# Half of a depthwise convolution moved from VectorE to TensorE, with shifted copies of its input stacked on the partitions

## The chip, the cores and the metric

One core of one Trainium2 chip runs the whole program. The metric is the device time of one execution in microseconds (us), as the median over runs.

## The reference, cut to what matters

The program chains two transformer-like blocks over 256 tokens with 2048 channels. The second block has four layers; the third of them (one of four) mixes with a gated convolution along the tokens. Only that layer is touched:

```python
def conformer_conv_mix(h, w_in, dw_w, dw_b, ln_g, ln_b, w_out):
    a, a_gate, z = jnp.split(h @ w_in, 3, axis=-1)          # 2048 -> 3 x 2048
    g = a * jax.nn.sigmoid(a_gate)
    # depthwise: 31 taps along the tokens, one weight per tap and channel, pad 15
    y = lax.conv_general_dilated(g, dw_w[:, None, :], (1,), [(15, 15)], ..., 
                                 feature_group_count=2048) + dw_b
    y = jax.nn.silu(layer_norm(y, ln_g, ln_b))
    return (y * jax.nn.silu(z)) @ w_out
```

## The kernel before, in words

Channels lie on the 128 partitions, in 16 blocks of 128 channels, and the 256 tokens lie on the free axis. All large projections run alike. The weights come from HBM in slabs of 1 MB (128 partitions x 2048 float32), four slabs to a *group* of four output blocks. SyncE loads each slab into one of four `raw` buffers. Every product is made to nearly float32 precision from three fp32r matmuls: ScalarE casts the slab to `whi` (L942, two buffers, so that the cast of a slab waits until the slab two places earlier has been multiplied), VectorE subtracts to get `wlo` (L1372), and TensorE runs 48 matmuls per slab (L456, L457, L458: high x high, high weights x low input, low weights x high input), 192 per group. The instruction order of each engine is written out by hand, and semaphores tie the engines together.

In the convolution layer the first projection is called `ci` and has 12 groups. Groups 0 to 7 each give two channel blocks of `a` and two of `a_gate`; ScalarE makes the sigmoid (L1314) and VectorE the product, into `gp` (L1973, `drain_ci`), which is padded by 15 zero tokens on both sides. Groups 8 to 11 give `z`. The convolution is done by VectorE alone, in 16 blocks x 31 taps = 496 instructions on 128 x 256 elements: `conv_steps` yields them two blocks at a time, and `conv_some(17)` puts 17 of them behind the drain, behind the third and behind the fourth weight subtraction of every group:

```python
for g in range(1, 12):
    split(r, g, 0)
    split(r, g, 1)
    if g <= 8:
        drain_ci(g - 1)
    conv_some(17)
    split(r, g, 2)
    conv_some(17)
    split(r, g, 3)
    conv_some(17)
```

When group 10 has been multiplied, TensorE sums the convolved blocks over the channels for the layer norm (L867, plain float32 matmuls with a matrix of ones); it waits there for all 16 blocks (`s_conv`). Then follow group 11, the sum of squares (L875), the normalization, and the projection `co`. GpSimd only issues DMAs: the modulation weights `w["ada"]`, 512 KB each (L430), which VectorE sums (L1398) in those stages that have `ada` work; `ci` has none.

Of the kernel before, what the change touches and what calls it, by code (L numbers as in the profile page):

```python
# [21 lines left out]
ACT = mybir.ActivationFunctionType  # L22
# [128 lines left out]
def build(nc, w, vec, out):  # L151
    ctx = ExitStack()
    with ctx:
# [3 lines left out]
        def sb(name, cols, dt=F32, at=None):  # L157
            nonlocal base
            if at is None:
                at = base  # L160
                base += (cols * 4 + 31) // 32 * 32
            place[name] = at
            return nc.alloc_sbuf_tensor_at(name, [P, cols], dt, offset=at)

        def sem(name):
            return ctx.enter_context(nc.semaphore(name))
# [67 lines left out]
        kc = tiles(sb("kc", 4 * T, at=arena + 36864))  # L234
        vx = tiles(sb("vx", 2 * T, at=arena + 40960))
        vc = tiles(sb("vc", 2 * T, at=arena + 43008))
        PADT = T + 30
        gp_t = sb("gp", KT * PADT, at=arena)
        gp = gp_t[:, :].rearrange("p (k n) -> p k n", n=PADT)
        zs_t = sb("zs", KT * T, at=arena + KT * PADT * 4)  # L240
# [1 line left out]
        yc_t = sb("yc", KT * T, at=arena + KT * PADT * 4 + 16384)  # L242
        yc = tiles(yc_t)
        k2 = sb("k2", K2_N, at=arena + 52224)
        assert arena + 52224 + K2_N * 4 <= 229368 and base <= 229368, (base, arena)
        dft = k2[:, K2_DFT:K2_DFT + 1024].rearrange("p (k n) -> p k n", k=2)
        chan = k2[:, K2_CHAN:K2_CHAN + 512].rearrange("p (k n) -> p k n", k=2)
# [72 lines left out]
        s_f2 = sem("dft_even_odd_ready")  # L320
        s_fe = sem("dft_even_copied")
        s_fb = sem("dft_combined")
        s_cg = sem("conv_gates_ready")
        s_conv = sem("conv_done")
        s_lnq = sem("conv_squares_ready")
# [21 lines left out]
        def gate_halves(r, q):  # L347

            n = 8 * (2 + r["extra"])
            return range(min(n, (3 + (not r["extra"])) * q // 2), min(n, (3 + (not r["extra"])) * (q + 1) // 2))  # L350

        def gate_sums(r, q):

            return [h // 8 for h in gate_halves(r, q - 3) if h % 8 == 7] if q >= 3 else []

        def conv_squares(c):
            return (sq[:, 0:1024], sq[:, 1024:2048], pt[:, :], sq[:, 0:1024])[c]
# [59 lines left out]
        @block.gpsimd  # L417
        def _(pool):
            nc.gpsimd.memset(ones[:, :], 1.0).then_inc(s_const, 1)

            def load(a, i, both):

                per = 4 if both else 2
                if i >= 2:
                    pool.wait_ge(s_acc, ada_at(a, both) + per * (i - 1))
                elif not isinstance(a, int) or a:
                    before = both or isinstance(a, int)
                    pool.wait_ge(s_acc, ada_at(a, both) - ((4 if before else 2) * (1 - i) + (not before)))
                pool.dma_start(aslab[:, i % 2, :, :].rearrange("p k n -> p (k n)"),  # L430
                               w["ada"][a, i // 2, :, 1024 * (i % 2):1024 * (i % 2) + 1024])\
                    .then_inc(s_araw[i % 2], 16)

            def group(a, both):
                for i in range(8):
                    load(a, i, both)
            group(0, True)
            with pool.Fori(1, ADA_BOTH) as a:
                group(a, True)
            group(ADA_BOTH, False)  # L440
            with pool.Fori(ADA_BOTH + 1, ADA_GROUPS) as a:
                group(a, False)

# [3 lines left out]
        def _(pe):  # L448
# [409 lines left out]
            project("ao", "ya")  # L858

            norm("nci")  # L860
            project("ci", "nci", n=10)
            project("ci", None, g0=10, n=1)

            for c in range(4):
                pe.wait_ge(s_conv, 4 * c + 4)
                for k in range(4):
                    last = nc.tensor.matmul(bank[5][:, 0:T], ones[:, :], yc[:, 4 * c + k, :],  # L867
                                            start=c == 0 and k == 0, stop=c == 3 and k == 3)
            last.then_inc(s_lns, 1)
            project("ci", None, g0=11, n=1)  # L870

            for c in range(4):
                pe.wait_ge(s_lnq, c + 1)
# [61 lines left out]
        def _(act):  # L935
            def split(r, g, s):
                act.wait_ge(s_raw[s], (g + (r["m0"] + 1)) * 16)
                n = r["width"]
                m = g * SLABS + (SLABS * r["m0"] + s)
                if not (isinstance(m, int) and m < 2):  # L940
                    act.wait_ge(s_slab, m - 1)
                nc.scalar.copy(whi[:, s % 2, 0:n], raw[:, s, 0:n]).then_inc(s_hi, 1)  # L942
# [365 lines left out]
            def drain_ci(r, g, par):  # L1308
                summed(r, g)
                if g < 8:  # L1310

                    if g >= 2:
                        act.wait_ge(s_drain, 2 * (r["e0"] + g - 1))
                    nc.scalar.activation(sq[:, 1024 * (g % 2):1024 * (g % 2) + 512],  # L1314
                                         bank[2 * par + 1][:, :], ACT.Sigmoid).then_inc(s_cg, 1)
                else:
                    if g == 8:

                        act.wait_ge(s_drain, 2 * (r["e0"] + 8))
                    for half in range(2):  # L1320
                        at = 1024 * (g - 8) + 512 * half
                        last = nc.scalar.activation(zs_t[:, at:at + 512], bank[2 * par + half][:, :],
                                                    ACT.Silu)
                    last.then_inc(s_drain, 2)
            split(r, 0, 2)
            split(r, 0, 3)
            for g in range(1, 12):
                split(r, g, 0)
                split(r, g, 1)
                drain_ci(r, g - 1, (r["e0"] + g - 1) % 2)  # L1330
                split(r, g, 2)
                split(r, g, 3)
            for c in range(4):
                act.wait_ge(s_lnr, c + 1)
                if c == 3:
                    act.wait_ge(s_lns, 2)
                nc.scalar.activation(conv_squares(c), yc_t[:, 1024 * c:1024 * c + 1024],
                                     ACT.Square).then_inc(s_lnq, 1)
                if c == 2:
                    drain_ci(r, 11, (r["e0"] + 11) % 2)  # L1340
# [18 lines left out]
        def _(dve):  # L1359
# [577 lines left out]

            def conv_steps():

                for k in range(0, KT, 2):  # L1940
                    for t in range(TAPS):
                        for b in (k, k + 1):
                            x = gp[:, b, t:t + T]
                            wt = col("conv_dw_w_2", 16 * t + b)
                            yield b, t, x, wt
# [33 lines left out]
            for g in range(1, 12):  # L1979
                split(r, g, 0)  # L1980
                split(r, g, 1)
                if g <= 8:
                    drain_ci(g - 1)
                conv_some(17)
                split(r, g, 2)
                conv_some(17)
                split(r, g, 3)
                conv_some(17)
            dve.wait_ge(s_lns, 1)
            mu = sc[:, 512:768]  # L1990
            link(v.tensor_scalar(mu, bank[5][:, 0:T], 1.0 / D, None, ALU.mult))
# [58 lines left out]
def host_weights(a):  # L2050
# [47 lines left out]
    out["wao"] = slabs_of(a["attn_w_out_2"][0], full)  # L2098
    ci = [c for g in range(8) for c in (256 * g, 256 * g + P, D + 256 * g, D + 256 * g + P)]
    out["wci"] = slabs_of(a["conv_w_in_2"][0], ci + run_of(2 * D, 16))  # L2100
    out["wco"] = slabs_of(a["conv_w_out_2"][0], full)
    return out

# [90 lines left out]
```

## Time and profile before

| what | us |
|---|---|
| median of 3 runs (lowest, highest) | 3667.39 (3663.97, 3670.04) |
| the profiled execution, its own time | 3667.97 |
| its span in the trace | 3666.3 |
| TensorE matmul busy / share | 3333.8 / 91% |
| VectorE busy / share | 2686.8 / 73% |
| granted TensorE clock, mean | 0.945 |
| groups 1 to 10 of `ci` | 2873.6 to 3172.0 |

### The profile page before, as it was taken

The numbers are of one execution on the slowest core, as the hardware profiler recorded it, in microseconds if no ns is written. First come the engines' busy times: TensorE is split into PE (matmuls) and PEld (weight loads), VectorE is DVE, ScalarE is ACT, GpSimd is POOL, SyncE is SP. The second block draws the span as 40 slices with busy tenths as digits, with TensorE's granted clock in tenths as the row PEclk, the third lists the DMA queues.
The fourth block names the chain that finished last, engine by engine and source line by source line (L and its number), as shares of the span: only waits on it lengthen the run. The fifth ranks groups of instructions, "written<-read, shape, count | busy, mean of one in ns | idle before, by whom it ended". The sixth has DMA issues, their size and how long they took to land.

```text
span 3666.3 us, 59897 instructions
## 1 busy us (share of the span) xinstructions
PE 3333.8 (91%) x24466; PEld 3131.4 (85%) x24466; DVE 2686.8 (73%) x3615; ACT 1371.6 (37%) x1506; POOL 203.6 (6%) x389
## 2 busy tenths in 40 slices
PE   5999788999998789989999999898999888989998
PEld 5999657989996569979999999897779878889998
DVE  7887777888886778876767576566776899767554
ACT  3333334343333343343333334433553322344332
POOL 0000000000000000000100010000000000000000
PEclk9999878999998779999999999999999999999999
DMA  5777304757776017756776675574007344456753
GB/s 207 260 262 255 134 12 161 253 199 265 262 261 209 23 59 263 253 197 226 254 260 223 212 260 202 176 268 174 1 12 264 127 139 139 147 197 222 236 186 137
DMA packets 124954, 696.51 MB, mean 190 GB/s; under 512 B 14136, under 2 KB 14288, under 8 KB 66128
## 3 DMA queue, kind: packets, MB, share of 16 engines
q1 hardware_dynamic: 67392, 484.47, 38.3%
q0 software_dynamic: 55296, 201.35, 15.4%
q10 hardware_dynamic: 2064, 7.78, 0.6%
q8 instruction: 152, 2.49, 0.3%
q14 instruction: 50, 0.41, 0.0%
HBM read 691.43 MB, written 2.10 MB: 189 GB/s over the span
## 4 chain that ended last, share of the span: by engine, by line
PE 72%; DVE 18%; ACT 4%; issue 3%; DMA 3%; ACTq 0%; DVEq 0%; POOLq 0%
PE bank L456 19%; PE bank L457 18%; PE bank L458 18%; DVE wlo L1372 4%; DVE yc L1962 4%; DMA aslab<-w_ada_dram 2%; ACT whi L942 2%; PE bank L559 2%; DVE acc L1398 2%; PE bank L853 2%; PE bank L550 1%; DVE sc L1531 1%; PE bank L790 1%; PE bank L769 1%; PE bank L834 1%
## 5 line engine op out<-in xcount | busy, mean ns | idle before, releaser
L456 PE MATMUL bank<-uhi,whi 128*128 128x256 f32 x6784 | 1960.1, 289 | 180.0 <-DVE wlo L1372 89.6
L457 PE MATMUL bank<-ulo,whi 128*128 128x256 f32 x6784 | 1941.3, 286 | 0.0
L458 PE MATMUL bank<-uhi,wlo 128*128 128x256 f32 x6784 | 1940.2, 286 | 0.0
L942 ACT CAST whi<-raw 128x2048 fp32r<-128x2048 f32 (+1 forms) x464 | 875.6, 1889 | 1786.1 <-PE bank L458 1710.7
L1372 DVE TENSOR_TENSOR wlo<-raw,whi 128x2048 fp32r<-128x2048 f32 (+1 forms) x464 | 1054.0, 2273 | 649.1 <-ACT whi L942 648.9
L456 PEld LDWEIGHTS bank<-uhi,whi 128*128 128x128 f32 x6784 | 1325.0, 195 | 196.7 <-issue 129.0
L457 PEld LDWEIGHTS bank<-ulo,whi 128*128 128x128 f32 x6784 | 1325.9, 195 | 1.0
L458 PEld LDWEIGHTS bank<-uhi,wlo 128*128 128x128 f32 x6784 | 1324.3, 195 | 0.0
L1398 DVE SCALAR_TENSOR_TENSOR acc<-aslab,sm,acc 128x512 f32<-128x512 f32 x1008 | 695.9, 747 | 58.1 <-DMA aslab<-w_ada_dram 57.7
L430 POOL DMA_DIRECT2D aslab<-w_ada_dram x384 | 203.2, 529 | 3299.0 <-DVE acc L1398 2528.6
L1962 DVE SCALAR_TENSOR_TENSOR yc<-gp,cols,yc 128x256 f32<-128x256 f32 x480 | 193.3, 489 | 0.0
L559 PE MATMUL bank<-sq,ones 128*128 128x256 f32 x160 | 47.6, 461 | 39.7 <-ACT sq L1022 39.7
L1295 ACT ACTIVATE sc<-sc,sm 128x512 f32<-128x512 f32 x64 | 46.2, 722 | 96.7 <-DVE sm L1901 96.7
L494 PE MATMUL bank<-whi,uhi 128*128 128x512 f32 (+1 forms) x192 | 71.0, 370 | 10.9 <-DVE wlo L1372 7.9
L1169 ACT ACTIVATE sc<-sc,sm 128x256 f32<-128x256 f32 x84 | 42.0, 501 | 101.8 <-DVE sm L1757 101.8
L559 PEld LDWEIGHTS bank<-sq,ones 128*128 128x128 f32 x160 | 36.7, 236 | 47.6 <-issue 31.2
L1505 DVE RECIPROCAL sc<-sc 128x256 f32<-128x256 f32 x10 | 17.5, 1753 | 79.2 <-ACT sc L1030 79.2
L1893 DVE SCALAR_TENSOR_TENSOR sc<-bank,k 128x512 f32<-128x512 f32 x64 | 44.3, 692 | 40.1 <-PE bank L836 40.1
L496 PE MATMUL bank<-wlo,uhi 128*128 128x512 f32 (+1 forms) x192 | 69.6, 363 | 0.0
L498 PE MATMUL bank<-whi,ulo 128*128 128x512 f32 (+1 forms) x192 | 69.4, 361 | 0.0
L550 PEld LDWEIGHTS bank<-ones,asum 128*128 128x128 f32 x576 | 69.0, 192 | 0.4
L550 PE MATMUL bank<-ones,asum 128*128 128x1 f32 x576 | 67.0, 243 | 0.0
(249 smaller groups left out, 2607.7 us busy)
## 6 DMA issues: line engine op xcount, KB each, us to landing
aslab<-w_ada_dram POOLq DMA_DIRECT2D x384, 512.0 KB, 5.3
raw<-w_win_dram SPq DMA_DIRECT2D x96, 1024.0 KB, 5.0
raw<-w_wfi_dram SPq DMA_DIRECT2D x96, 1024.0 KB, 5.7
raw<-w_wfo_dram SPq DMA_DIRECT2D x48, 1024.0 KB, 5.0
raw<-w_wci_dram SPq DMA_DIRECT2D x48, 1024.0 KB, 4.9
raw<-w_wo_dram SPq DMA_DIRECT2D x32, 1024.0 KB, 4.9
raw<-w_wpg_dram SPq DMA_DIRECT2D x32, 1024.0 KB, 5.2
raw<-w_wqz_dram SPq DMA_DIRECT2D x32, 1024.0 KB, 5.1
```

The lines of the kernel that those rows point to most:

```text
L430: pool.dma_start(aslab[:, i % 2, :, :].rearrange("p k n -> p (k n)"), w["ada"][a, i // 2, :, 1024 * (i % 2):1024 * (i % 2) + 1024])\
L456: nc.tensor.matmul(o, whi_, xhi_, start=start, stop=False, skip_group_check=True)
L457: nc.tensor.matmul(o, whi_, xlo_, start=False, stop=False, skip_group_check=True)
L458: return nc.tensor.matmul(o, wlo_, xhi_, start=False, stop=stop, skip_group_check=True)
L494: nc.tensor.matmul(o, uhi[:, kt, tk], whi[:, s % 2, wc], start=kt == 0, stop=False, skip_group_check=True)
L550: last = nc.tensor.matmul(o, asum[:, c, P * b:P * (b + 1)], ones[:, 0:1], start=True, stop=True, skip_group_check=True)
L559: last = nc.tensor.matmul(bank[7][:, 0:T], ones[:, :], squares(c)[:, T * k:T * (k + 1)], start=c == 0 and k == 0, stop=c == 3 and k == 3)
L853: last = nc.tensor.matmul(o, v, p[:, P * c:P * (c + 1)], start=c == 0, stop=c == 3, skip_group_check=True)
L942: nc.scalar.copy(whi[:, s % 2, 0:n], raw[:, s, 0:n]).then_inc(s_hi, 1)
L1372: v.tensor_tensor(wlo[:, s, 0:n], raw[:, s, 0:n], whi[:, s % 2, 0:n].bitcast(F32), ALU.subtract).then_inc(s_lo, 1)
L1398: ins = v.scalar_tensor_tensor(out=out, in0=x, scalar=silu, in1=before, op0=ALU.mult, op1=ALU.add)
L1962: ins = v.scalar_tensor_tensor(out=yc[:, b, :], in0=x, scalar=wt, in1=yc[:, b, :], op0=ALU.mult, op1=ALU.add)
```

## The change

Of every four channel blocks, VectorE keeps the first two (0, 1, 4, 5, 8, 9, 12, 13) and TensorE takes the other two (`PE_BLOCKS`: 2, 3, 6, 7, 10, 11, 14, 15).

For each of TensorE's blocks GpSimd issues 17 DMAs: one of 512 KB from HBM with the tap matrices, made on the host (`wcv`), and 16 from SBUF to SBUF of 32 partitions x 284 float32 (36 KB), which write four copies of `gp`, shifted by 0, 1, 2 and 3 tokens, below one another on the partitions, once for each quarter (32 channels) of the block. A contraction over the 128 partitions then covers four taps of 32 channels. TensorE multiplies in 8 steps of four taps with four matmuls each (one per quarter, 128 x 32 weights, 256 tokens, plain float32), each writing its own 32 partitions of the same PSUM bank (6 or 7): 32 matmuls per block. The buffers for taps and shifted copies are double. ScalarE copies the result to `yc` and adds the bias. A block is multiplied behind the second and another behind the fourth slab of groups 3, 5, 7 and 9; TensorE's groups are no longer in a hardware loop there. VectorE's share per group goes from 17+17+17 to 10+9+9 instructions. GpSimd's loop over the modulation loads is cut in two, and the loads for `co` are issued after those of the convolution.

```diff
-        PADT = T + 30
+        PADT = T + 32
+        SHIFT = T + 28
+        shifted = [k2[:, K2_AX:K2_AX + 4 * SHIFT], zs_t[:, 2048:2048 + 4 * SHIFT]]
+        taps = [pt[:, :], sc[:, 0:1024]]
+        PE_BLOCKS = [4 * (i // 2) + 2 + i % 2 for i in range(8)]
 # GpSimd
-            with pool.Fori(ADA_BOTH + 1, ADA_GROUPS) as a:
+            with pool.Fori(ADA_BOTH + 1, RUN["co"]["a0"]) as a:
+                group(a, False)
+            pool.wait_ge(s_nl, 16 * (U_NORMS["nci"] + 1))
+            for i, b in enumerate(PE_BLOCKS):
+                if i >= 2:
+                    pool.wait_ge(s_cp, i - 1)
+                pool.dma_start(taps[i % 2], w["wcv"][i]).then_inc(s_cl_[i % 2], 16)
+                pool.wait_ge(s_drain, 2 * (RUN["ci"]["e0"] + b // 2 + 1))
+                for j in range(4):
+                    for c in range(4):
+                        pool.dma_start(shifted[i % 2][32 * j:32 * j + 32, SHIFT * c:SHIFT * (c + 1)],
+                                       gp[32 * c:32 * c + 32, b, j:j + SHIFT]).then_inc(s_cl_[i % 2], 16)
+            with pool.Fori(RUN["co"]["a0"], ADA_GROUPS) as a:
                 group(a, False)
 # TensorE
-            project("ci", "nci", n=10)
-            project("ci", None, g0=10, n=1)
+            def conv_block(i):
+                pe.wait_ge(s_cl_[i % 2], 16 * 17 * (i // 2 + 1))
+                if i >= 2:
+                    pe.wait_ge(s_cc, i - 1)
+                for q in range(8):
+                    for c in range(4):
+                        at = 32 * (4 * q + c)
+                        last = nc.tensor.matmul(bank[6 + i % 2][32 * c:32 * c + 32, 0:T],
+                                                taps[i % 2][:, at:at + 32],
+                                                shifted[i % 2][:, SHIFT * c + 4 * q:SHIFT * c + 4 * q + T],
+                                                start=q == 0, stop=q == 7, skip_group_check=True)
+                last.then_inc(s_cp, 1)
+            def behind(g, s):
+                if g in (3, 5, 7, 9) and s % 2:
+                    conv_block(g - 3 + s // 2)
+            for g in range(11):
+                group(r, g, (r["e0"] + g) % 2, slab_t, "nci" if g == 0 else None,
+                      lambda s, g=g: behind(g, s))
             for c in range(4):
-                pe.wait_ge(s_conv, 4 * c + 4)
+                pe.wait_ge(s_conv, 2 * c + 2)
+                pe.wait_ge(s_cc, 2 * c + 2)
 # ScalarE
+            def conv_copy(i):
+                act.wait_ge(s_cp, i + 1)
+                b = PE_BLOCKS[i]
+                nc.scalar.activation(yc[:, b, :], bank[6 + i % 2][:, 0:T], ACT.Identity,
+                                     bias=col("conv_dw_b_2", b)).then_inc(s_cc, 1)
             for g in range(1, 12):
                 split(r, g, 0)
                 split(r, g, 1)
+                if g in (4, 6, 8, 10):
+                    conv_copy(g - 3)
                 drain_ci(r, g - 1, (r["e0"] + g - 1) % 2)
                 split(r, g, 2)
                 split(r, g, 3)
+                if g in (3, 5, 7, 9):
+                    conv_copy(g - 3)
 # VectorE
-                for k in range(0, KT, 2):
+                for k in range(0, KT, 4):
                     for t in range(TAPS):
                         for b in (k, k + 1):
...
-                conv_some(17)
+                conv_some(10)
                 split(r, g, 2)
-                conv_some(17)
+                conv_some(9)
                 split(r, g, 3)
-                conv_some(17)
+                conv_some(9)
```

## Rows read from the trace of the kernel before

**Rows 1.** The page: span, busy engines, shares of the chain that ended last.

```profile
span 3666.3 us, 59897 instructions
PE 3333.8 (91%) x24466; PEld 3131.4 (85%) x24466; DVE 2686.8 (73%) x3615; ACT 1371.6 (37%) x1506; POOL 203.6 (6%) x389
...
PE 72%; DVE 18%; ACT 4%; issue 3%; DMA 3%; ACTq 0%; DVEq 0%; POOLq 0%
```

**Rows 2.** Stretches: an `in0` group, `ci` group 0, groups 1 to 10, one group, L867, tail.

```profile
core 0: us, PE busy (x) PEld busy (x) DVE busy (x) ACT busy (x) POOL busy (x), PEclk, DMA share, GB/s
184.00:207.00 23.00, 23.00 (x195) 23.00 (x194) 18.24 (x19) 7.03 (x6) 1.72 (x4) 1.00 0.73 265
2847.30:2873.60 26.30, 25.58 (x195) 25.41 (x196) 17.69 (x26) 10.76 (x15) 0.00 (x0) 0.91 0.35 120
2873.60:3172.00 298.40, 249.89 (x1920) 244.65 (x1919) 289.17 (x544) 84.87 (x54) 0.00 (x0) 0.95 0.41 141
2934.00:2964.20 30.20, 25.30 (x192) 24.69 (x192) 29.56 (x57) 8.11 (x5) 0.00 (x0) 0.94 0.41 140
3172.00:3179.00 7.00, 7.00 (x35) 6.17 (x34) 2.29 (x1) 2.88 (x3) 0.00 (x0) 1.00 0.46 152
3202.10:3224.70 22.60, 6.91 (x32) 5.74 (x32) 16.73 (x13) 19.22 (x27) 0.00 (x0) 0.75 0.14 46
```

**Rows 3.** Waits in `ci` groups 1 to 10 (us in total, times, longest).

```profile
ACT whi L942 <- PE bank L458: 211.7, 40, 8.5
...
PE bank L456 <- DVE wlo L1372: 45.4, 24, 2.9
DVE wlo L1372 <- ACT whi L942: 8.2, 9, 3.5
```

**Rows 4.** VectorE in order of time, over one group of `ci` (start us, us).

```profile
2966.17 2.29 DVE L1372 TENSOR_TENSOR wlo<-raw,whi 128x2048 fp32r<-128x2048 f32 x1 [0.65 <-ACT whi L942]
2968.38 0.69 DVE L1973 TENSOR_TENSOR gp<-bank,sq 128x512 f32<-128x512 f32 x1
2968.98 6.82 DVE L1962 SCALAR_TENSOR_TENSOR yc<-gp,cols,yc 128x256 f32<-128x256 f32 x17
2975.70 2.29 DVE L1372 TENSOR_TENSOR wlo<-raw,whi 128x2048 fp32r<-128x2048 f32 x1
...
2993.42 2.30 DVE L1372 TENSOR_TENSOR wlo<-raw,whi 128x2048 fp32r<-128x2048 f32 x1
2996.43 2.29 DVE L1372 TENSOR_TENSOR wlo<-raw,whi 128x2048 fp32r<-128x2048 f32 x1 [0.71 <-ACT whi L942]
```

**Rows 5.** TensorE in order of time around L867.

```profile
3171.77 0.28 PE L457 MATMUL bank<-ulo,whi 128*128 128x256 f32 x1
3171.89 0.28 PE L458 MATMUL bank<-uhi,wlo 128*128 128x256 f32 x1
3172.01 7.07 PE L867 MATMUL bank<-yc,ones 128*128 128x256 f32 x32
3178.72 0.47 PE L456 MATMUL bank<-uhi,whi 128*128 128x256 f32 x1
```

**Rows 6.** TensorE at 466 us: the first two index heads, float32, 64 partitions each.

```profile
466.92 1.14 PE L625 MATMUL bank<-zz 64*128 64x256 f32 x8 [2.61 <-DVE an L1563]
```

**Rows 7.** TensorE: one-column matmuls, each with its own 128x128 weights.

```profile
3273.53 0.95 PE L550 MATMUL bank<-ones,asum 128*128 128x1 f32 x8
```

**Rows 8.** TensorE in the attention, where the shape of the tile changes.

```profile
2660.38 0.60 PE L853 MATMUL bank<-pt,vc 128*64 128x128 f32 x4
2660.91 0.70 PE L834 MATMUL bank<-kx,zq 64*128 64x256 f32 x2
2661.45 0.59 PE L836 MATMUL bank<-kc,zq 64*128 64x256 f32 x2
2661.97 0.66 PE L843 MATMUL bank<-kk,sc 128*128 128x128 f32 x4
```

**Rows 9.** GpSimd: its two DMAs back to back, and DMA issues of the page.

```profile
1.42 1.19 POOL L430 DMA_DIRECT2D aslab<-w_ada_dram  x2 [0.34 <-issue]
...
aslab<-w_ada_dram POOLq DMA_DIRECT2D x384, 512.0 KB, 5.3
```

**Rows 10.** ScalarE in order of time: casts around the end of `ci` group 3.

```profile
2964.24 1.90 ACT L942 CAST whi<-raw 128x2048 fp32r<-128x2048 f32 x1 [8.38 <-PE bank L458]
2966.04 0.59 ACT L1314 ACTIVATE sq<-bank 128x512 f32<-128x512 f32 x1
2971.68 1.91 ACT L942 CAST whi<-raw 128x2048 fp32r<-128x2048 f32 x1 [5.04 <-PE bank L458]
```

**Rows 11.** Smallest ScalarE operation of the shape that the new copy has.

```profile
2840.76 0.47 ACT L1030 ACTIVATE sc<-bank,sm 128x256 f32<-128x256 f32 x1 [1.96 <-PE bank L559]
```

**Rows 12.** SyncE's loads during one `ci` group.

```profile
q1 hardware_dynamic: 576, 4.19, 40.6%
...
raw<-w_wci_dram SPq DMA_DIRECT2D x4, 1024.0 KB, 4.9
```

More of the change, by code:

```diff
@@ L244, in build @@
         k2 = sb("k2", K2_N, at=arena + 52224)
+        SHIFT = T + 28
+        shifted = [k2[:, K2_AX:K2_AX + 4 * SHIFT], zs_t[:, 2048:2048 + 4 * SHIFT]]
+        taps = [pt[:, :], sc[:, 0:1024]]
+        assert K2_AX + 4 * SHIFT <= K2_N and KT * PADT * 4 + 2 * 16384 <= 52224
         assert arena + 52224 + K2_N * 4 <= 229368 and base <= 229368, (base, arena)
@@ L322, in build @@
         s_fb = sem("dft_combined")
+        s_cl_ = [sem(f"conv_shifts_and_taps_loaded{i}") for i in range(2)]
+        s_cp = sem("conv_block_multiplied")
+        s_cc = sem("conv_block_copied")
         s_cg = sem("conv_gates_ready")
@@ L860, in _ @@
             norm("nci")
-            project("ci", "nci", n=10)
-            project("ci", None, g0=10, n=1)
+            r = RUN["ci"]
+            def conv_block(i):
[16 more added lines that the diff above has]
+                      lambda s, g=g: behind(g, s))
             for c in range(4):
-                pe.wait_ge(s_conv, 4 * c + 4)
+                pe.wait_ge(s_conv, 2 * c + 2)
+                pe.wait_ge(s_cc, 2 * c + 2)
                 for k in range(4):
@@ L869, in _ @@
             last.then_inc(s_lns, 1)
-            project("ci", None, g0=11, n=1)
+            group(r, 11, (r["e0"] + 11) % 2, slab_t)
             for c in range(4):
@@ L1319, in drain_ci @@
                         act.wait_ge(s_drain, 2 * (r["e0"] + 8))
+                    if g == 10:
+                        act.wait_ge(s_cp, 8)
                     for half in range(2):
@@ L2100, in host_weights @@
     out["wci"] = slabs_of(a["conv_w_in_2"][0], ci + run_of(2 * D, 16))
+    dw = np.asarray(a["conv_dw_w_2"][0])
+    taps = np.zeros((8, P, 8, 4, 32), dw.dtype)
+    lane = np.arange(32)
+    for i in range(8):
+        b = 4 * (i // 2) + 2 + i % 2
+        for t in range(dw.shape[0]):
+            for c in range(4):
+                taps[i, 32 * (t % 4) + lane, t // 4, c, lane] = dw[t, P * b + 32 * c + lane]
+    out["wcv"] = taps.reshape(8, P, 1024)
     out["wco"] = slabs_of(a["conv_w_out_2"][0], full)
```

## The prediction

> **What bounds the kernel now.** The page says that TensorE is the fullest engine and holds 72% of the chain that ended last, VectorE 18% [rows 1]. An average does not say who is late in `ci`, so the stretches come next. The bound elsewhere is an `in0` group: 192 fp32r matmuls, each 0.12 us behind the last [rows 5], take 192 x 0.12 = 23.04 us, and the stretch shows TensorE busy for all of its 23.0 us [rows 2]. Groups 1 to 10 of `ci` take 298.4 us instead of 230.4, at a clock of 0.95 instead of 1.00, and VectorE is busy for 289.2 of them (97%) [rows 2]. The waits agree: TensorE waits 45.4 us for `wlo` from VectorE, while VectorE waits 8.2 us for anything [rows 3]. The rest of the 68.0 us (298.4 - 230.4) is restarts and slabs that run at the lower clock after a wait. So `ci` is bound by VectorE, and 68.0 us is all that a lighter VectorE can give back there.
>
> VectorE's group of 30.2 us is, by starts in [rows 4], four subtractions at 2.21 us (8.8), one drain at 0.60 and 51 convolution steps at 6.72/17 = 0.396 us (20.2), with about 0.6 of waiting: 29.6 + 0.6. The pitch of 0.396, not the duration, is the price, since the instructions overlap.
>
> **What is removed.** 248 of 496 steps x 0.396 = 98 us of VectorE. A group's load becomes 8.8 + 0.6 + 28 x 0.396 (11.1) = 20.5 us, under TensorE's 23.04. Work is left for 248/28 = 8.9 groups, so VectorE ends in group 9, before L867. The later a subtraction may come counts too: a cast takes 1.9 us and a subtraction 2.3 behind the end of the slab two back, and TensorE needs it 5.76 us (23.04/4) after that end. A chunk of 10 steps (4.0) plus one subtraction (2.2) is 6.2, 0.4 over 5.76, and the chunks of 9 are 5.8; the 1.5 us in hand absorbs both. The `in0` stretch has almost this load, 18.2 us busy on VectorE in gaps of 2.7 us, and shows no TensorE idle [rows 2]. So the bound passes to TensorE, and I let VectorE's steps cost nothing behind it; should that cover fail, rival C prices it. For restarts and uneven chunks I allow 0.25 us a group, 2.5 us; this is a choice, about the size of one late restart (0.31 us from L456 to L457 after L867 where 0.12 is the rule).
>
> **What is added on TensorE.** This is the term that decides. Eight blocks of 32 float32 matmuls, two records each, are 64 records a block. A float32 record of 256 tokens starts 6.71/31 = 0.216 us after the last at clock 1.00 [rows 2, 5]. If the four 32-column tiles take turns, a block is 64 x 0.216 = 13.8 us; if all four run at once, 16 x 0.216 = 3.5 us, a pitch of 0.054 us per record. The trace has no adjacent column tiles. It has row tiles: heads 0 and 1 of L625 sit on partitions 0 to 63 and 64 to 127, and their 8 records take 1.14 us with the last one's 0.38 inside, (1.14 - 0.38)/7 = 0.109 us of pitch, half of 0.216 [rows 6]. So float32 matmuls on different parts of the array do overlap. Against a full factor of four stand the weights: 8 one-column matmuls, each with a fresh 128-column load, have a pitch near (0.95 - 0.25)/7 = 0.10 us [rows 7], which would make 64 records 6.4 us; here a load is 32 columns, a quarter. Bounds of the block are thus 3.5 and 13.8, with 6.4 between them. I take a pitch of 0.066 us (4.2 us), close to the end of four at once, because the nearest row [rows 6] halves exactly and the load shrinks with its columns. Changing the tile shape costs about 0.1 us each way: L834 begins 0.20 us after the last record of L853 where that one's pitch is 0.11 [rows 8]; with the first, longer matmul I add 0.3. A block is 4.5 us, eight are 36 us, all on the path, since nothing else can run on TensorE.
>
> The Trainium skill (TensorE: Matmul & The Clock Gate, Measured speedup vs the span model) reports 2.38x for three column tiles of 32 columns; that is 79% of full, and an estimate from the page at the same share would be 3.2x for four, 4.4 us for 64 records. No run here shows column tiles yet; by the page the sum would be 2 us longer.
>
> **What is added elsewhere.** ScalarE gets eight copies of about 0.5 us [rows 11] in a stretch where it is busy 85 of 298 us [rows 2]. In line behind a copy stand the sigmoid, the drain and the next cast; the copy of an odd block waits for the block that TensorE runs first anyway, so the cast behind it is due only after another 5.76 us slab [rows 10]. Nothing. The other end, 8 x 0.5 = 4 us, is inside the range.
>
> GpSimd issues 17 DMAs a block, idle otherwise. Two 512 KB DMAs back to back took 1.19 us together, so 0.66 a piece [rows 9]; for 17, 11 us, plus a landing of at most 5.3 [rows 9]. A pair of blocks is needed once in two groups, 46 + 9 = 55 us. Blocks 2 and 3 are drained about 5 us into group 2 and wanted 11.5 and 23 us into group 3: 29 us for the first, against 11 + 5. Hidden up to about 1.4 us per DMA (34 x 1.4 + 5.3 + some 2 for the waits between = 55). The `ada` loads for `co` come behind them on GpSimd's queue, in group 9 at the latest, over 40 us before `co` wants them. The transfers add 8 x (0.5 + 0.57) = 8.6 MB to queues at 41% in this stage [rows 12]; `in0` ran at 73% without delaying TensorE [rows 2]. Nothing. Group 0 (26.3 us), L867 (7 us), group 11 and the tail (22.6 us with TensorE mostly idle) [rows 2] stay.
>
> **Sum.** Groups 1 to 10: 230.4 + 36.0 + 2.5 = 268.9 us against 298.4, 29.5 us less. The profiled execution had 3667.97 us, 1.7 outside its span of 3666.3, and lies 0.6 above the median, so the difference is taken from the median: 3667.4 - 29.5 = 3638 us (-0.8%). Break-even is a block of 65.5/8 = 8.2 us, a pitch of 0.123, or 1.75 tiles at once.
>
> **Rivals.**
> - A, column tiles take turns (slower). Each matmul uses all 128 partitions, so the load for the next tile or the stream of the moving operand could exclude the other tiles; the only overlap seen is between different partitions [rows 6]. Then a block is 13.8 + 0.3 = 14.1, eight 113 us: 230.4 + 113 + 2.5 = 346, 47 us more, 3715 us. It decides from 8.2 us per block. For it: no row shows column tiles side by side. Against: the array's parts do work independently. The Trainium skill (TensorE: Matmul & The Clock Gate, The mechanism) states that weight loads overlap running matmuls only when the row group differs, which speaks for this rival; here loads of 0.19 us run under matmuls of the same rows at a pitch of 0.12, so the trace does not bear it out for whole tiles. Chance 0.13.
> - B, they overlap by halves, or the weight loads set the pace at 0.10 to 0.11: a block of about 7 us, 56 us in all, 10 us faster, 3658 us. Chance 0.12.
> - C, VectorE stays late: its in-order chunks delay subtractions by 0.5 us on each of the 40 slabs, 20 us of the gain: 3656. The `in0` stretch speaks against it. Chance 0.06.
> - D, GpSimd's gathers are late. From 1.4 us per DMA the 34 of a pair exceed the 55 us, and each further 0.1 us costs 4 x 3.4 = 14 us; at 1.6 the gain is gone, at 2 it is 6 x 14 - 29.5 = 54 us slower, 3722. Against: 0.66 for larger ones [rows 9]. For: no SBUF to SBUF DMA of this size is in the trace. Chance 0.06, half of it slower.
>
> The forecast, 0.63. Its own range is a block of 3.8 to 5.5 us with 0 to 4 us of waits: 3630 to 3648.
>
> **How the numbers follow.** Faster by over 0.2% (7.3 us, about what a measurement of this kernel can tell from no change, its runs spreading over 6): 0.63 + 0.10 of B + 0.06 of C + 0.01 of D = 0.80. Slower: A 0.13, D 0.03 = 0.16. Between: 0.04. The low end of the range is the full factor of four and no waits, 230.4 + 8 x 3.6 = 259, 39 us less: 3628. The high end takes in B and C, 3660, and leaves A and most of D out.
>
> **What would show it.** Right: the records of the new matmuls at a pitch of 0.05 to 0.08 us, blocks of 4 to 5.5 us, no wait of TensorE on `wlo` over 1 us in even groups, VectorE near 20.5 us busy per group, L867 about 29 us earlier, GpSimd done with a block before TensorE asks. Wrong: a pitch of 0.2 (A) or 0.1 (B), waits on `wlo` (C), a wait on a DMA in front of a block (D), or a clock below 1.00 in `ci`, which would stretch everything on TensorE.

## The result

| | before | changed |
|---|---|---|
| median, us (lowest to highest) | 3668.7 (3663.97 to 3670.04, 4 runs) | 3621.11 (3613.81 to 3624.17, 4 runs) |
| ratio of the times, 95% interval | | 0.987 (0.9852 to 0.9887) |
| the profiled execution, its own time / span | 3667.97 / 3666.3 | 3622.15 / 3620.5 |
| mean granted TensorE clock | 0.945 | 0.949 |

Faster, as forecast, but by 47.6 us where 29.5 were worked out: the time lies below the low end of the range (3628). The direction and the place were right, two terms were too dear, and some microseconds came from outside the stage, where the prediction counted nothing.

**Where the time went.** The page of the changed kernel, for [rows 1]: VectorE has lost 97 us of work, and its share of the chain has fallen from 18% to 13%.

```profile
span 3620.5 us, 60788 instructions
PE 3340.4 (92%) x24978; PEld 3130.4 (86%) x24978; DVE 2589.8 (72%) x3367; ACT 1375.8 (38%) x1514; POOL 270.6 (7%) x525
...
PE 79%; DVE 13%; ACT 3%; issue 3%; DMA 2%; ACTq 0%; DVEq 0%; POOLq 0%
```

Stretches of the changed kernel, for [rows 2]: group 0 of `ci`, and groups 1 to 10 with the eight blocks.

```profile
core 0: us, PE busy (x) PEld busy (x) DVE busy (x) ACT busy (x) POOL busy (x), PEclk, DMA share, GB/s
2839.50:2865.90 26.40, 25.49 (x195) 25.35 (x196) 17.78 (x26) 10.87 (x15) 0.53 (x1) 0.92 0.40 140
2865.90:3126.50 260.60, 260.60 (x2433) 246.60 (x2433) 192.76 (x296) 88.62 (x63) 67.60 (x137) 1.00 0.61 198
```

Groups 1 to 10 take 260.6 us instead of 298.4, TensorE is busy for all of them, and the clock is 1.00 where it was 0.95. The queues moved 198 GB/s and TensorE waited for none of it. Behind it stand the matmuls of the layer norm (L910, L867 before), as in [rows 5]:

```profile
3126.24 7.07 PE L910 MATMUL bank<-yc,ones 128*128 128x256 f32 x32
```

The waits in that stretch, for [rows 3]: TensorE has none, for `wlo` or for a DMA; its weight loads show 3.3 us of issue, the rest are waits of engines that have time. VectorE's for ScalarE went from 8.2 to 66.6 us: it is now the one that waits.

```profile
engine line waited for: us in total, times, longest us
ACT whi L985 <- PE bank L480: 162.4, 41, 5.5
POOL k L461 <- DVE gp L2027: 92.4, 4, 42.8
DVE wlo L1426 <- ACT whi L985: 66.6, 21, 7.3
POOL pt L457 <- PE bank L893: 55.2, 3, 20.4
ACT yc L1375 <- PE bank L893: 13.3, 8, 1.7
PEld bank L478 <- issue: 3.3, 8, 0.4
```

**The price of a block.** ScalarE casts once per slab, so the pitch of its casts is the time of a slab, and of a slab with a block behind it. ScalarE in order of time (start us, us):

```profile
2917.69 1.90 ACT L985 CAST whi<-raw 128x2048 fp32r<-128x2048 f32 x1 [3.36 <-PE bank L480]
2923.45 1.90 ACT L985 CAST whi<-raw 128x2048 fp32r<-128x2048 f32 x1 [3.85 <-PE bank L480]
2927.01 0.48 ACT L1375 ACTIVATE yc<-bank,cols 128x256 f32<-128x256 f32 x1 [1.67 <-PE bank L893]
2932.99 1.90 ACT L985 CAST whi<-raw 128x2048 fp32r<-128x2048 f32 x1 [5.50 <-PE bank L480]
```

2923.45 - 2917.69 = 5.76 us is a bare slab; 2932.99 - 2923.45 = 9.54 is one with a block: the block costs **3.78 us**. TensorE over the same block:

```profile
2923.08 0.28 PE L480 MATMUL bank<-uhi,wlo 128*128 128x256 f32 x1
2923.28 3.66 PE L893 MATMUL bank<-k,pt 128*32 128x256 f32 x64
2926.88 0.39 PE L478 MATMUL bank<-uhi,whi 128*128 128x256 f32 x1
2927.10 0.28 PE L479 MATMUL bank<-ulo,whi 128*128 128x256 f32 x1
```

Its first four records alone, in a shorter stretch:

```profile
2923.28 0.42 PE L893 MATMUL bank<-k,pt 128*32 128x256 f32 x4
```

64 records with the last one's 0.38 inside: (3.66 - 0.38)/63 = 0.052 us of pitch. The first four are over in 0.42 us, where one alone takes 0.40: they run together. Record by record the rest does the same: four start within 0.02 us (2926.115, .121, .128, .135) and the next four 0.216 later, 16 steps x 0.2155 = 3.45, and 0.33 is left of the 3.78 for the edges. All four column tiles run at once, and between the edges nothing is lost. The weight loads (128 x 32) take 0.11 us each, four of them start within 0.02 us as well, and all lie under the matmuls. With 8 x 3.78 = 30.2, groups 1 to 10 should take 230.4 + 30.2 = 260.6 us, which is what they take.

**GpSimd**, in order of time: 16 gathers in 7.83 us, 0.49 each.

```profile
2944.37 7.83 POOL L461 DMA_DIRECT2D k<-gp  x16 [16.52 <-DVE gp L2027]
2952.18 0.57 POOL L457 DMA_DIRECT2D sc<-w_wcv_dram  x1
2952.75 7.82 POOL L461 DMA_DIRECT2D zs<-gp  x16
```

And when they land (page, KB each, median us to landing):

```profile
k<-gp POOLq DMA_DIRECT2D x64, 35.5 KB, 3.4
zs<-gp POOLq DMA_DIRECT2D x64, 35.5 KB, 5.5
```

The last shift for `k` is issued before 2952.2 and lands at 2956.7; TensorE multiplies them from 2976.93, 20.2 us later. Over the eight blocks the least margin is that of the first, 15.4 us.

From the start of `ci` to the start of `co` (VectorE's first subtraction of each) it is 377.62 us before and 339.57 after: **38.05 us less**. The other 8 us of the difference between the two traces are no part of this stage: `ci` began at 2829.2 us in one and at 2821.5 in the other. The experiments take up both.

### The profile page after: what moved, and what is told of

Read it like the earlier page. It is cut to its first block, busy times and chain, and to the rows that moved or that the text cites. A ratio compares the mean times of both kernels' runs of the same rounds, so it can differ in the third digit from the quotient of the medians.

```text
span 3620.5 us, 60788 instructions
## 1 busy us (share of the span) xinstructions
PE 3340.4 (92%) x24978; PEld 3130.4 (86%) x24978; DVE 2589.8 (72%) x3367; ACT 1375.8 (38%) x1514; POOL 270.6 (7%) x525
## 4 chain that ended last, share of the span: by engine, by line
PE 79%; DVE 13%; ACT 3%; issue 3%; DMA 2%; ACTq 0%; DVEq 0%; POOLq 0%
PE bank L478 21%; PE bank L479 20%; PE bank L480 20%; DVE wlo L1426 3%; PE bank L581 2%; DMA aslab<-w_ada_dram 2%; DVE acc L1452 2%; PE bank L875 2%; ACT whi L985 2%; PE bank L572 1%; DVE sc L1585 1%; PE bank L812 1%; PE bank L791 1%; PE bank L856 1%; PE bank L865 1%
## 5 line engine op out<-in xcount | busy, mean ns | idle before, releaser
L2016 DVE SCALAR_TENSOR_TENSOR yc<-gp,cols,yc 128x256 f32<-128x256 f32 x240 | 97.4, 476 | 0.0
L581 PEld LDWEIGHTS bank<-sq,ones 128*128 128x128 f32 x160 | 35.2, 226 | 47.6 <-issue 32.8
```

Source lines behind the costliest of these rows:

```text
L581: last = nc.tensor.matmul(bank[7][:, 0:T], ones[:, :], squares(c)[:, T * k:T * (k + 1)], start=c == 0 and k == 0, stop=c == 3 and k == 3)
L2016: ins = v.scalar_tensor_tensor(out=yc[:, b, :], in0=x, scalar=wt, in1=yc[:, b, :], op0=ALU.mult, op1=ALU.add)
```

## The experiments

"Stage" is the time from the start of `ci` to the start of `co` in the profiled execution. The kernel before was run 15 to 17 times beside each set of experiments; all its runs, 70 with the four of the result, have a mean of 3665.7 us.

| run | `ci` starts | stage | stage against before | median (runs) | ratio to before |
|---|---|---|---|---|---|
| before | 2829.2 | 377.62 | | | |
| changed | 2821.5 | 339.57 | -38.05 | 3621.11 (4) | 0.9870 |
| e1 before, extra input | 2826.2 | 377.38 | -0.2 | 3664.58 (11) | 0.9998 |
| e2 changed again | 2831.7 | 339.57 | -38.05 | 3623.75 (4) | 0.9878 |
| e3 six blocks | 2825.9 | 334.21 | -43.4 | 3620.27 (4) | 0.9876 |
| e4 quarter outer | 2822.7 | 402.30 | +24.7 | 3685.72 (5) | 1.0057 |
| e5 half left out | 2826.2 | 309.33 | -68.3 | 3596.64 (5) | 0.9807 |
| e6 before, written out | 2820.7 | 377.66 | 0.0 | 3660.31 (12) | 0.9988 |
| e7 one tile | 2822.0 | 422.28 | +44.7 | 3703.95 (4) | 1.0096 |
| e8 gathers in quarters | 2821.1 | 420.42 | +42.8 | 3700.20 (4) | 1.0093 |
| e9 changed, looped | 2830.3 | 339.58 | -38.0 | 3624.46 (4) | 0.9887 |
| e10 as e6 | 2821.0 | 377.60 | 0.0 | 3660.10 (12) | 0.9987 |
| e11 as e3 | 2818.8 | 334.21 | -43.4 | 3622.71 (4) | 0.9888 |
| e12 one step | 2820.5 | 315.35 | -62.3 | 3594.81 (4) | 0.9813 |
| e13 `qz` written out | 2825.3 | 376.96 | -0.7 | 3664.52 (12) | 1.0000 |
| e14 changed again | 2820.3 | 339.58 | -38.0 | 3620.24 (4) | 0.9884 |
| e15 as e9 | 2830.7 | 339.58 | -38.0 | 3625.50 (5) | 0.9897 |

### What the stage can give back: e5

The kernel before with half of the convolution left out (blocks 2, 3, 6, 7, 10, 11, 14, 15 are filled with a constant), nothing put on TensorE:

```diff
-                for k in range(0, KT, 2):
+                for k in range(0, KT, 4):
...
-                conv_some(17)
+                conv_some(10)
```

The other two chunks of a group become 9 and 9; as in the change, GpSimd's loop over the modulation loads is cut in two.

> The kernel before with half of the convolution left out: VectorE makes blocks 0, 1, 4, 5, 8, 9, 12 and 13 in chunks of 10, 9 and 9, GpSimd fills the others with a constant, TensorE takes nothing over. This is what the change removes, by itself. If the stage is bound by VectorE alone, groups 1 to 10 fall from 298.4 to 230.4 us (TensorE's own pace) and the whole to 3601 us or less, with no wait of TensorE on wlo. If chunks of 10 in VectorE's order still delay the subtractions, the groups take 24 us or more each. If the changed program gains 5 us outside the stage through something that this edit shares (GpSimd's order, the chunks), it shows here as well.

The ten groups after group 0, as one stretch:

```profile
core 0: us, PE busy (x) PEld busy (x) DVE busy (x) ACT busy (x) POOL busy (x), PEclk, DMA share, GB/s
2858.80:3089.20 230.40, 230.40 (x1920) 230.40 (x1921) 191.86 (x296) 84.25 (x54) 0.53 (x1) 1.00 0.54 187
```

10 groups in exactly 230.4 us at clock 1.00, with no gap. The stage is 68.3 us shorter, and the prediction's 68.0 are all there. Rival C (VectorE's chunks delay subtractions, 20 us) is out, and so are the 2.5 us allowed for restarts: VectorE's chunks of 10, 9 and 9 leave TensorE no gap.

### The order of the matmuls: e4 and e7

e4 swaps the two loops of a block, so that the eight steps of one quarter follow each other; e7 lets all 32 matmuls write the same 32 partitions of PSUM (the sum of the four quarters instead of the quarters).

```diff
# e4
-                for q in range(8):
-                    for c in range(4):
+                for c in range(4):
+                    for q in range(8):
# e7
-  nc.tensor.matmul(bank[6 + i % 2][32 * c:32 * c + 32, 0:T],
+  nc.tensor.matmul(bank[6 + i % 2][0:32, 0:T],
```

> The same 32 matmuls of a block, but all eight steps of one quarter before the next quarter, so that neighbours in the program use the same column tile. If the overlap needs neighbours on different tiles, a block takes 64 x 0.216 = 13.8 us and the stage grows by 8 x 10.3 = 82 us: 3703 us. If TensorE looks ahead as far as it did for the two index heads (four records), quarters overlap in part: a block between 4 and 10 us. If it looks ahead over the whole block, nothing changes.

> The changed kernel with all 32 matmuls of a block sent to the same 32 PSUM partitions, so that no two column tiles can overlap; the convolution of TensorE's blocks is wrong by that. This prices rival A. Expected: 64 records at 0.216 us, a block of 13.8 + 0.3 = 14.1 us instead of 3.78, the stage 82 us longer: about 3705 us. If the overlap had another cause than the column tiles (small weights, the shape), the block stays near 3.8.

One block on TensorE in e7, all 64 records in one row:

```profile
2923.79 14.00 PE L893 MATMUL bank<-k,pt 128*32 128x256 f32 x64
```

(14.00 - 0.38)/63 = 0.216 us: one after the other, the price of rival A (14.1 a block), and with it the stage is 44.7 us longer where 8 x 14.1 - 68 = 45 are worked out. Here too every matmul has new weights, loaded in 0.11 us under the 0.216 of the record before. The same block in e4, then two cuts out of it, one inside a quarter and one where the quarter changes:

```profile
2924.52 11.50 PE L893 MATMUL bank<-k,pt 128*32 128x256 f32 x64
...
2924.52 1.91 PE L893 MATMUL bank<-k,pt 128*32 128x256 f32 x8
...
2926.70 1.70 PE L893 MATMUL bank<-k,pt 128*32 128x256 f32 x11
```

Inside a quarter the pitch is (1.91 - 0.38)/7 = 0.219; where it changes, (1.70 - 0.38)/10 = 0.132. By their starts, four records of the old quarter and four of the new one run in pairs at each of the three changes, and all others alone: 64 - 12 = 52 steps x 0.2155 + 0.33 = 11.5 us. So here a record of the next tile started at most four records ahead of its turn. With the steps outside (the change) the next tile is always that near; with the quarters outside it is so at three places only, 12 pairs in 64 records, and the kernel is slower than before. The block of 11.5 us is above the 4 to 10 that the expectation gave this case. How far TensorE reaches ahead in orders other than these two was not tried.

### The block's price by its length: e12

Only the first of the eight steps is multiplied (4 of 32 matmuls, the other 28 taps of these blocks left out), everything else unchanged:

```diff
-                for q in range(8):
+                for q in range(1):
```

> The changed kernel whose blocks multiply only the first of the eight groups of four taps: 4 matmuls a block instead of 32, the other 28 taps of these blocks are left out. Theory (a block is 8 x 0.43 us of matmuls, four tiles at once, and 0.33 us of edges): a block is 0.43 + 0.33 = 0.76 us, groups 1 to 10 take 230.4 + 8 x 0.76 = 236.5 us if neither VectorE nor the gathers bind, 24 us less than the change, about 3597 us. Rival (with TensorE this light, VectorE's chunks or the gathers of GpSimd come next): waits of TensorE for `wlo` or for a DMA, and a stage over 320 us.

ScalarE's casts around one such block:

```profile
2922.50 1.91 ACT L985 CAST whi<-raw 128x2048 fp32r<-128x2048 f32 x1 [3.84 <-PE bank L480]
2924.32 0.46 ACT L1375 ACTIVATE yc<-bank,cols 128x256 f32<-128x256 f32 x1
2929.02 1.91 ACT L985 CAST whi<-raw 128x2048 fp32r<-128x2048 f32 x1 [4.24 <-PE bank L480]
```

6.52 - 5.76 = 0.76 us, as expected, and the stage is 24.2 us below the change's. A block is 0.33 us of edges plus 0.43 for each step of four matmuls. The 17 DMAs of each block still run, and TensorE waits for none, nor for `wlo`.

### Six blocks: e3 and e11

TensorE takes 6 blocks, VectorE 10, in chunks of 11, 10 and 10.

```diff
-        PE_BLOCKS = [4 * (i // 2) + 2 + i % 2 for i in range(8)]
+        PE_BLOCKS = [4 * (i // 2) + 2 + i % 2 for i in range(6)]
...
-                for k in range(0, KT, 4):
+                for k in (0, 4, 8, 12, 14):
```

> TensorE takes six blocks instead of eight (2, 3, 6, 7, 10, 11), VectorE ten, in chunks of 11, 10 and 10. If TensorE is now the only bound, groups 1 to 10 fall from 260.6 to 230.4 + 6 x 3.78 = 253.1 us, with up to 2 us of waiting at the channel sums because VectorE ends in group 10: 5 to 7.5 us faster than the change, about 3615. If VectorE, at 8.8 + 0.6 + 31 x 0.396 = 21.7 us a group, is late with subtractions, TensorE waits on wlo in most groups and its clock falls: no gain, or 3620 to 3630.

> Six blocks on TensorE and ten on VectorE, as in e3, whose stage was 5.4 us shorter than the change's and whose time was within 1 us of it. Theory (a block is 3.78 us of TensorE, two fewer save 7.6 us less some 2 us of late subtractions): 5 us below the change in the stage again and 3616 us, ratio 0.986. Rival (VectorE, now with 31 steps a group, gives it back): the change's 3621 us.

The stage is 334.21 us in both traces, 5.4 less than the change's: two blocks are 7.6 us, and 2.2 come back, because VectorE now has 31 steps a group. They come back at six slabs, 0.2 to 0.5 us each. Five lie in the groups before the first block, where nothing on TensorE gives VectorE time to catch up; ScalarE's casts in e3, each 5.76 us behind the last where nothing is late, show two of them (6.01 and 6.16 us):

```profile
2881.81 1.91 ACT L985 CAST whi<-raw 128x2048 fp32r<-128x2048 f32 x1 [3.85 <-PE bank L480]
2887.82 1.91 ACT L985 CAST whi<-raw 128x2048 fp32r<-128x2048 f32 x1 [4.10 <-PE bank L480]
2893.98 1.91 ACT L985 CAST whi<-raw 128x2048 fp32r<-128x2048 f32 x1 [4.25 <-PE bank L480]
```

That part is settled. The time of the whole did not follow: e3 and e11 together have a mean of 3620.4 us over 8 runs (standard error 1.2), the change 3621.2 over 12 (1.4), a difference of 0.8 +- 1.8 where 5.4 were expected. `ci` begins and the kernel ends in the two profiled executions as in those of the change, so nothing there takes 4 us back. Whether the six-block kernel is really faster stays open; no run shows it slower. The last experiments come back to it.

### The gathers: e8

The 16 gathers of a block cut into 64 of 8 partitions each, 65 DMAs a block instead of 17 for the same bytes.

```diff
                 for j in range(4):
                     for c in range(4):
+                      for p in range(0, 32, 8):
-                        pool.dma_start(shifted[i % 2][32 * j:32 * j + 32, ...
+                        pool.dma_start(shifted[i % 2][32 * j + p:32 * j + p + 8, ...
```

> The changed kernel with each of the 16 gathers of a block cut into four of 8 partitions: 65 DMAs a block instead of 17, the same bytes. In the trace of the change GpSimd starts one every 0.49 us. Rival D says that GpSimd becomes the bound when a pair of blocks costs it more than the 53.6 us that TensorE needs for two groups and two blocks. 130 x 0.49 = 64 us plus landing: 10 to 16 us late per pair in three or four pairs, 35 to 60 us in all: 3655 to 3680 us, with TensorE waiting on DMAs in front of odd blocks. If a smaller DMA is cheaper for GpSimd (a quarter of the rows), it stays hidden and nothing changes.

GpSimd, then TensorE in front of a block and in it (L894 here, L893 in the change), then the clock in the same stretches:

```profile
2928.43 31.47 POOL L462 DMA_DIRECT2D zs<-gp  x64
...
2969.49 31.49 POOL L462 DMA_DIRECT2D k<-gp  x64 [9.04 <-DVE gp L2028]
```

```profile
3034.35 5.50 PE L894 MATMUL bank<-zs,sc 128*32 128x256 f32 x64 [15.52 <-DMA zs<-gp]
```

```profile
core 0: us, PE busy (x) PEld busy (x) DVE busy (x) ACT busy (x) POOL busy (x), PEclk, DMA share, GB/s
3020.00:3034.30 14.30, 0.00 (x0) 0.00 (x0) 2.29 (x1) 0.82 (x1) 13.72 (x28) 0.54 0.29 91
3034.30:3040.00 5.70, 5.65 (x65) 2.72 (x66) 0.00 (x0) 0.07 (x1) 0.00 (x0) 0.66 0.28 95
3040.00:3046.00 6.00, 6.00 (x52) 6.00 (x52) 4.65 (x11) 1.01 (x3) 4.03 (x9) 1.00 0.05 9
```

31.47/64 = 0.49 us for 9 KB, the same as for 36 KB: GpSimd's price is per DMA, not per byte. 130 DMAs a pair of blocks are 64 us, more than the 55 there are, and TensorE waits 70.1 us for the two buffers in all:

```profile
PE bank L894 <- DMA zs<-gp: 59.0, 4, 15.5
PE bank L894 <- DMA k<-gp: 11.1, 4, 6.9
```

That is more than the 35 to 60 expected. In front of each pair GpSimd also waits for `gp` (9.04 us above), which VectorE drains only when TensorE has done its group: a pair costs GpSimd 72.5 us (2969.49 to 3041.97) and not 64. After such a wait of 15.5 us the granted clock is 0.54, the lower level (1.2 GHz), and the records of the block come in fours 0.43 apart instead of 0.216 until it is back at 1.00: 5.50 us instead of 3.66. The stage is 80.9 us over the change's: 70.1 of it is waits, and five of the eight blocks run in part at the lower clock (6.48, 6.29, 5.50, 5.20 and 5.04 us), 10.2 us more together. So rival D is a real mechanism, with its threshold between 17 and 65 DMAs a block; at 17 the gathers have at least 15 us in hand.

### What lies ahead of `ci`: e1, e2, e6, e9, e10, e13, e14, e15

The stage gives 38.05 us in every trace of the change; the times differ by more. The change also adds 4 MB of input, and it writes TensorE's program of `ci` out where before it was a hardware loop. e1 gives the kernel before an unused input of that size; e2 and e14 are the change again.

> The kernel before, with one more input of 4 MB in HBM that nothing reads (the size of the tap matrices). The convolution stage saved 37.8 us in the first trace of the change, and the rest of the 47.6 us lies ahead of it, in code that did not change: `ci` began 7.7 us earlier. If the extra input moves the other tensors in HBM so that loads land sooner (5.2 instead of 5.7 us for w_wfi), this kernel gains the same 8 to 10 us: about 3660 us, ratio 0.998. If it is the spread between executions, or the layout of the program, this kernel takes 3668 us, ratio 0.999 to 1.001.

> The changed kernel once more, unaltered. If the 7.7 us ahead of `ci` are spread between executions, `ci` begins anywhere from 2821 to 2830 us in the new trace and the median lies between 3618 and 3630. If they belong to the change (its program or its data in HBM), `ci` begins within 2 us of 2821.5 again and the difference to the kernel before is 45 to 50 us. The stage itself should repeat: groups 1 to 10 in 260.6 us, eight blocks of 3.78 us.

e1: 0.9998 (0.9989 to 1.0008). So it is not an input of that size by itself. e2 (0.9878, 0.9861 to 0.9894) shows how loosely one trace tells this: the same program began `ci` 10 us later than in its first trace, with the stage equal to 0.01 us.

e6 and e10 write out the kernel before; e9 and e15 put groups 5 to 10 of the changed one back into a loop; e13 writes out the stage `qz` of the kernel before instead of `ci`.

```diff
# e6, e10
-            project("ci", "nci", n=10)
-            project("ci", None, g0=10, n=1)
+            for g in range(11):
+                group(r, g, (r["e0"] + g) % 2, slab_t, "nci" if g == 0 else None)
# e9, e15
-            for g in range(11):
+            for g in range(5):
                 group(r, g, (r["e0"] + g) % 2, slab_t, "nci" if g == 0 else None,
                       lambda s, g=g: behind(g, s))
+            with pe.Fori(1, 4) as j:
+                group(r, j * 2 + 3, (r["e0"] + 3) % 2, slab_t, None,
+                      lambda s: conv_block(s // 2, j) if s % 2 else None)
+                group(r, j * 2 + 4, (r["e0"] + 4) % 2, slab_t)
# e13
-            project("qz", None)
+            for g0 in range(0, 8, 2):
+                project("qz", None, g0=g0, n=2)
```

> The kernel before with TensorE's ci groups written out one by one, as in the change, and nothing else. The stage is bound by VectorE, so it should keep its 298.4 us. The changed kernel gains 45 us in the median, its stage 38; if the other 5 to 7 us come from the longer program of TensorE, they appear here: 3660 us, ratio 0.998 to 0.9985. If they are spread between executions, the ratio is 0.9995 to 1.0005.

> The changed kernel, whose TensorE program of the stage `ci` is a hardware loop again from group 5 to group 10 (two groups and two blocks of the convolution a turn); the work is the same. Theory 1 (the 4 to 6 us that the change gains outside the stage come from the TensorE program of `ci` being written out, as e6 suggests with its ratio of 0.9988): the stage from the start of `ci` to the start of `co` stays at 339.6 us, `ci` begins 3 to 6 us later, the median is 3625 to 3628. Rival (they are the spread of one execution from the next, and the stage's 38 us are the lower half of what it brings): no difference from the change, 3621 us. Second rival: a branch of the loop costs something at each turn, seen as gaps of TensorE at the start of every second group.

> The kernel before with TensorE's groups of `ci` written out, once more as in e6 (0.9988, interval 0.9978 to 0.9999). Theory 1 (written out, the program gains something ahead of `ci`): a ratio near 0.9988 again, about 4 us below the kernel before, stage unchanged at 377.7 us. Rival (nothing but spread): a ratio of 1.000 within 0.001.

> The kernel before, whose TensorE program of the stage `qz` (8 groups, the last stage but one ahead of `ci`) is written out, and `ci` left as the loop that it was. Theory 1 (what gains 4 to 5 us in e6 and e10 is that TensorE's program is longer by some 1200 matmuls, wherever they stand): a ratio near 0.999 here too, with `ci` beginning below 2824 us in the trace. Rival (it hangs on the loop of `ci` itself, or is spread): 1.000 within 0.001, and `ci` begins at 2826 to 2830 us as in the other programs with a loop there.

> The changed kernel unaltered, beside e15 on the same chip. Expected: 3621 us as in the earlier runs (3613 to 3630), stage `ci` 38.05 us shorter than before.

> The changed kernel with TensorE's groups 5 to 10 of `ci` in a loop again, as in e9, beside e14. Theory 1 (written out, TensorE's program gains 4 to 5 us ahead of `ci`): 3625 to 3626 us, over e14 by 3 to 5 us, `ci` beginning at 2826 us or later in the trace. Rival: no difference from e14 within 1.5 us of the means over e2, e9, e14 and e15.

| TensorE's `ci` | kernel before, mean us (runs) | changed kernel, mean us (runs) |
|---|---|---|
| in a loop | 3665.7 (70) | 3626.1 (e9, e15: 9) |
| written out | 3660.9 (e6, e10: 24) | 3621.2 (changed, e2, e14: 12) |
| difference | 4.8 | 4.9 (standard error 1.9) |

Either pair of programs has the same work and the same stage (377.6 and 339.6 us). e6 and e10 give 0.9988 (0.9978 to 0.9999) and 0.9987 (0.9976 to 0.9999) independently, e14 and e15 lie 5 us apart on one chip. So taking the loop of `ci` apart, and nothing else of the change, brings some 4.8 us. e13 has no gain (1.0000, 0.9991 to 1.0009): writing out another stage does nothing, and theory 1 of that run falls. Over the traces `ci` begins at 2828.0 us on the mean of the six with the loop (2825.3 to 2830.7) and at 2822.4 of the eleven without (2818.8 to 2831.7). The difference grows from the front: 1.3 us after 140 us of the trace, 5.3 at the start of `qz`, 490 us before `ci`, in instructions that are the same in both.

What the stage does not explain can also be read from all runs together: each run's time, less the stage of its program's trace, is the rest of the kernel.

| | runs | rest of the kernel, mean us (standard error) |
|---|---|---|
| loop: before, e1, e5, e9, e13, e15 | 107 | 3287.8 (0.4) |
| written out: changed, e2, e4, e6, e7, e8, e10, e12, e14 | 53 | 3282.3 (0.6) |
| written out, six blocks: e3, e11 | 8 | 3286.2 (1.2) |

The first two rows are 5.5 us apart. The third is the exception: the six-block kernel has no loop in `ci` either, and its rest is almost that of the programs with one. That is where its missing 4 us are, and it says that the loop is not all that decides. How a loop that TensorE reaches at 2.83 ms moves what it does before was not found; it stays open.

## Why the prediction came out as it did

**What bounds the kernel, and the 68 us: right.** e5 gives 68.3 us in the stage for "68.0 us is all that a lighter VectorE can give back there". Three steps of the sum failed, the first two in size, and all to the same side.

**The block, "I take a pitch of 0.066 us ... A block is 4.5 us": the first step that failed, in size.** The mechanism was right, the tiles run at once. The pitch is 0.052 and the block 3.78 us, the low bound (3.5) and 0.3 of edges: 8 x 0.72 = 5.8 us. [rows 6] had halved the pitch exactly for two row tiles and bore the right conclusion; the step away from the full factor of four was made for weight loads, which [rows 7] shows at 0.10 us one behind the other. The loads of different column tiles overlap one another and the matmuls, four of 0.11 us in every 0.216. The Trainium skill (TensorE: Matmul & The Clock Gate, Measured speedup vs the span model) gives its 2.38x for three tiles beside a formula for the span of one pack; the estimate of 4.4 us carried it over to a stream of packs, and that is not borne out here: the measured factor is 14.00/3.66 = 3.8 over the whole block and 4.0 between its edges. The Trainium skill's rule on the same page (The mechanism), that a weight load overlaps running matmuls only when the row group differs, is not borne out either: all four tiles use all rows, and their loads hide.

**"For restarts and uneven chunks I allow 0.25 us a group, 2.5 us": the second, too dear.** It was 0 (e5, and the change's own 260.6 us). VectorE waits for ScalarE in front of half of its subtractions (21 of 40, 66.6/21 = 3.2 us each), which is room that uneven chunks use up first. The 31 steps a group of e3 begin to cost, 2.2 us.

**"so the difference is taken from the median": the third, and the one that left the range.** The sum takes the 29.5 us of groups 1 to 10 for the whole difference. It says of the rest of the stage and of the tail that they stay, and that held (26.4 us for group 0, 7.07 for the matmuls of L867); what the edit does ahead of the stage it puts at nothing without a reason. Taking TensorE's loop apart was worth about 4.8 us there (e6 and e10 without the rest of the change, e9 and e15 against it). The stage alone would have given 3667.4 - 38.05 = 3629.3 us, inside the range. The profile of before could not show this effect, and its cause is open; a range that ends at the stage's best case had no room for it.

**The base.** The median of three runs, 3667.4, was 1.7 above the mean of 70. Together: 1.7 + 5.8 + 2.5 + 4.8 = 14.8 of the 17 us; about 0.2 is in the stage outside groups 1 to 10. The last 2 are not explained; they are little more than the standard error of the change's mean (1.4).

**Rivals.** A is the right price for a tile that must wait its turn (e7), and another loop order gives four fifths of it (e4, 11.5 of 14.0 us a block); it isn't what the change does. B and C are refuted by the records of the block and by e5. D appeared at four times the DMAs, and not at the change's own: 0.49 us each where 1.4 was its threshold. ScalarE's copies cost nothing, as said: the copy waits for the block (1.67 us), and the cast behind it then waits 5.50 us more for TensorE. The signs of being right came out for `wlo`, VectorE's load and the gathers; the block, 3.8 us, lay below its 4 to 5.5.

## What to carry to other kernels

An operation with few output channels per tile can be cheap on TensorE if four 128 x 32 tiles are issued in turn, step by step: the whole price is then the stream of one tile. Put the tile index in the innermost loop; the same matmuls with the tile index outside were three times dearer and turned a gain of 1.2% into a loss. When SBUF-to-SBUF gathers feed them, count the DMAs and not the bytes, and give a forecast some room for an edit that takes a loop apart, since that moved this kernel by 0.13% in instructions that it did not touch, for a reason not found.

## What the runs showed of the hardware

- Four plain float32 matmuls on adjacent column tiles, all with 128 rows, start within 0.02 us, four to every 0.216 us; 128 x 32 weight loads of 0.11 us cost nothing beside them.
- With all matmuls of one column tile in a row, a record of the next tile started at most four records ahead of its turn (e4, 11.5 us a block against 3.66 and 14.00).
- A DMA issued by GpSimd from SBUF to SBUF took 0.49 us of GpSimd, for 9 KB as for 36 KB, and 3.4 and 5.5 us (medians for the two buffers) to land.
- After TensorE had waited 15.5 us the clock stood at 1.2 GHz, and a block took 5.50 us instead of 3.66.
- Executions of one program start the same late stage up to 10 us apart, while its length repeats to 0.01 us in the changed kernel and to 0.06 in the one written out before (e6, e10): a difference in the stage could be read from one trace, a difference in the whole could not.
